# Query weights loaded in pieces of 32 partitions by 2048 columns in place of 128 partitions by 512 columns

## The reference

```
h = x + W_out(concat[A, B, C, D](rmsnorm(x) @ W_in))
x = h + PEER(rmsnorm(h));   y = rmsnorm(x)
```

```
q  = (x @ wq).reshape(n, 8, 2, 128)             # wq is 1024 x 2048
s1 = q[:, :, 0] . k1 ; s2 = q[:, :, 1] . k2     # 128 keys per half and head
# top 16 of each half, top 16 of the 256 sums -> 16 experts per token and head, softmax gates
out[t] = sum_s g[s] * gelu(u_tab[e[s]] . x[t]) * v_tab[e[s]]     # 16384 experts
```

## Time and profile before

| | |
|---|---|
| median of three runs | 1734.4 us (1732.55 to 1735.49) |
| the profiled execution, time of the whole run | 1734.5 us |
| its span | 1732.7 us |
| mean granted TensorE clock | 0.843 of full speed |
| VectorE busy | 1241.3 us, 72% |
| TensorE matmul busy | 1232.9 us, 71% |
| POOL busy | 910.8 us, 53% |
| ScalarE busy | 698.0 us, 40% |
| moved by DMA | 602.42 MB, mean 348 GB/s |

### The profile page before, as it was taken

One profiled execution on the slowest core, in us unless ns is written; L12 is line 12 of the kernel. 1 busy time (PEld: TensorE's weight loads), 2 busy tenths in 40 slices (PEclk: granted clock), 3 DMA queues, 4 the chain that ended last, 5 costly groups with the idle time before them and its releaser, 6 DMA issues.

```text
span 1732.7 us, 19380 instructions
## 1 busy us (share of the span) xinstructions
PE 1232.9 (71%) x5360; PEld 619.5 (36%) x5360; DVE 1241.3 (72%) x2955; ACT 698.0 (40%) x1986; POOL 910.8 (53%) x1134
## 2 busy tenths in 40 slices
PE   5997898567777767767976767675766667666555
PEld 4886766322333333322322323232322222222110
DVE  3568755688887877768586778676767777767774
ACT  3321113455444444334345445343433343434444
POOL 0155120467576566555366656555656655656762
PEclk9999899778899898878986778778888887768878
DMA  6321147999999999999799999999999999999996
GB/s 173 122 98 49 37 137 100 318 390 418 414 415 416 407 418 419 417 417 398 255 388 417 419 417 416 417 378 418 419 417 418 418 418 412 409 417 402 420 415 255
DMA packets 110636, 602.42 MB, mean 348 GB/s; under 512 B 24752, under 2 KB 27184, under 8 KB 43968
## 3 DMA queue, kind: packets, MB, share of 16 engines
q0 software_dynamic: 74880, 545.29, 76.8%
q1 hardware_dynamic: 35648, 55.90, 11.0%
HBM read 597.96 MB, written 3.19 MB: 347 GB/s over the span
## 4 chain that ended last, share of the span: by engine, by line
DMA 39%; PE 27%; DVE 15%; POOL 6%; ACT 5%; issue 5%; DVEq 3%; POOLq 0%; SPq 0%; ACTq 0%
DMA arena<-in_uv,arena 38%; PE ps L985 10%; DVE arena L1848 8%; PE ps L553 5%; POOL arena L2072 4%; DVE arena L1320 3%; DVEq L1317 3%; PE ps L600 2%; POOL arena L2071 2%; PE ps L906 2%; PE ps L591 2%; DVE arena L1326 2%; PE ps L613 1%; PE ps L925 1%; ACT arena L1284 1%
## 5 line engine op out<-in xcount | busy, mean ns | idle before, releaser
L985 PE MATMUL ps<-arena 128*64 128x512 f32 x2048 | 662.8, 782 | 407.9 <-ACT arena L1284 407.7
L1848 DVE CUSTOM_DVE_ANT_0 arena<-arena 128x1024 f32<-128x1024 f32 x520 | 641.0, 1234 | 303.8 <-DMA arena<-in_uv,arena 285.0
L2072 POOL DMA_INDIRECT arena<-in_uv,arena x520 | 622.7, 1198 | 90.5 <-POOL arena L2071 8.7
L2071 POOL TENSOR_TENSOR arena<-arena 1x1 f32<-1x1 f32 x520 | 207.1, 398 | 534.9 <-PE ps L985 404.8
L985 PEld LDWEIGHTS ps<-arena 128*64 128x64 f32 x2048 | 152.1, 166 | 798.2 <-ACT arena L1284 553.2
L1278 ACT ACTIVATE arena<-arena 128x1 f32<-128x1 f32 x520 | 105.3, 202 | 757.3 <-DVE arena L1848 755.8
L1284 ACT ACTIVATE arena<-arena 128x64 f32<-128x64 f32 (+1 forms) x520 | 181.5, 349 | 17.0
L1280 ACT ACTIVATE arena<-arena 128x1 f32<-128x1 f32 x520 | 153.2, 295 | 16.9
L1320 DVE TENSOR_TENSOR arena<-arena 128x512 f32<-128x512 f32 (+7 forms) x310 | 132.6, 429 | 28.1 <-ACT arena L1032 18.9
L553 PE MATMUL ps<-arena 128*128 128x264 f32 (+1 forms) x608 | 141.9, 389 | 0.7 <-DVE arena L1320 0.7
L906 PEld LDWEIGHTS ps<-arena 128*128 128x128 f32 x1024 | 121.9, 198 | 34.9 <-issue 33.4
(11 more groups left out here) (161 smaller groups left out, 973.8 us busy)
## 6 DMA issues: line engine op xcount, KB each, us to landing
arena<-in_win SPq DMA_DIRECT2D x38, 512.0 KB, 3.3
arena<-in_wqk SPq DMA_DIRECT2D x64, 256.0 KB, 7.5
arena<-in_uv,arena POOLq DMA_INDIRECT x520, 12.3
arena<-in_wout SPq DMA_DIRECT2D x16, 512.0 KB, 7.8
arena<-in_xp SPq DMA_DIRECT2D x4, 512.0 KB, 7.5
arena<-in_wqk SPq DMA_DIRECT2D x16, 128.0 KB, 9.5
out_yp<-arena SPq DMA_DIRECT2D x4, 512.0 KB
arena<-in_const SPq DMA_DIRECT2D x1, 928.0 KB, 4.5
```

The lines of the kernel that those rows point to most:

```text
L985: last = mm(ps[64 * q:64 * q + 64, b + c, :], diag[:, (s + q) % 8, :], ring[:, (s + q) % RING, D + 512 * c:D + 512 * c + 512], start=(s == ...
L1848: v.tensor_tensor_reduce(out=ring[:, s % RING, 0:D], in0=ring[:, s % RING, 0:D], in1=row, scale=1.0, scalar=0.0, op0=MUL, op1=ADD, accum_o ...
L2071: pool.tensor_tensor(carrier[:, 1:2], carrier[:, 0:1], carrier[:, 0:1], ALU.add).then_inc(S["carried"], 1)
L2072: pool.indirect_dma_start(out=ring[:, s % RING, :], out_offset=None, in_=a["uv"][:, :], in_offset=bass.IndirectOffsetOnAxis(ap=idx[:, t, s ...
```

## The change

A piece is now 32 partitions with all 2048 columns. It was 128 partitions with 512 columns. The number of pieces (4 per load), their bytes (256 KB), the waits before each and the semaphore counts are as they were, and so is the DMA of the keys.

```diff
@@ L465, load 0
             for k in range(4):
-                sp_.dma_start(wqk[:, 512 * k:512 * k + 512], a["wqk"][0][:, 512 * k:512 * k + 512]).then_inc(d_wqk, 16)
+                sp_.dma_start(wqk[32 * k:32 * k + 32, 0:2048], a["wqk"][0][32 * k:32 * k + 32, 0:2048]).then_inc(d_wqk, 16)
@@ L490, loads 1 to 15, in next_keys(n)
                     if u >= LEAD:
                         sp_.wait_ge(S["slot_used"], TOPK * (u - LEAD) + 2 + 2 * k)
-                    sp_.dma_start(wqk[:, 512 * k:512 * k + 512], a["wqk"][QLOADS[n]][:, 512 * k:512 * k + 512]).then_inc(d_wqk, 16)
+                    sp_.dma_start(wqk[32 * k:32 * k + 32, 0:2048], a["wqk"][QLOADS[n]][32 * k:32 * k + 32, 0:2048]).then_inc(d_wqk, 16)
```

## The result

The changed kernel takes 1789.66 us (median of 4 runs, 1786.59 to 1794.9) against 1734.95 us beside it. The ratio is 1.0312, 95% interval 1.0278 to 1.0347. The forecast was 1746 us with a range up to 1763 us. The direction was right and the size was not: 55 us were lost where 12 were forecast.

The account below looks back on a forecast made before the run. DMA engine time was taken to bound the kernel in the gather stretches. From 1734.5 us, - 3 for packets and + 15 for collisions gave 1746.5, stated as 1746 us; the 8-in-10 range was 1730 to 1763 us.

Parts of the forecast that it names:

- What bounds the kernel: Over 310 to 820 and 850 to 1650 us, DMA engine time added or saved moves the end one for one.
- Issue: The same 60 instructions of 0.33 us on the mostly idle SP queue behind the same waits: nothing either way.
- the wait for the weights: Queries waiting for a load: a piece would have to land 12 us later to be felt, so nothing.
- load 0: Issued at 245.0 to 246.7 us, before the first gather, its first product 31 us later: costed at nothing.
- Packets: Weight pieces as 32 runs of 8 KB instead of 128 of 2 KB, 6144 fewer packets: 3 us saved.
- The near row: Rate beside a load, 414 and 415 against 419 GB/s: 0.30 us lost per load, 4.5 us for 15.
- Collisions: DMA engines writing into the same 32 partitions hinder each other: 0.25 us per piece, 15 us for 60.
- half rate: Each of a DMA engine's two packets per piece takes 0.32 us more: 0.64 us per piece, 38 us for 15 loads.
- The signs: If pieces cost, stretches with a load fall to about 400 GB/s, the mean over 850 to 1650 us to about 405.
- full collisions: Rival: every packet of a piece, and gather packets into those partitions, at half rate: + 38 - 3, 1769 us; chance 0.09.
- The row of `ys`: Output at the end, 8 rows of 4 KB: 0.48 us per packet against 0.161 for `yp`, read as engines obstructing each other.
- only half of the DMA engines carry a piece: Rival: eight engines get four packets each, the lag hidden by waiting gathers: 1731.5 us; 0.32 together with the other no-collision rival.

Follow-up runs that it names:

- Half of the narrow loads: Changed kernel with narrow 32-partition pieces only in loads with odd n, the others as before the change: 1763.12 us, ratio 1.0151 to the kernel before.
- load 0 alone: Only the first load, issued before any gather, uses the narrow pieces; the other 15 are as in the kernel before: 1738.31 us, ratio 1.0004.
- spread kernel: Changed kernel with each piece on every fourth partition instead of 32 neighbours: 1734.26 us, ratio 0.9982 to the kernel before; again in 12 runs 1734.61 us, 0.9979.
- alternating order: Changed kernel with the four pieces of a load in the order 0, 2, 1, 3: 1786.9 us, ratio 1.0275 to the kernel before.

## Why the prediction was wrong, step by step

**What bounds the kernel: right.** DMA engine time in these stretches goes to the end one for one. 40.6 + 15.3 = 55.9 us more per engine stand beside 57.5 us more span, and the 51.4 us lost behind the loads beside 51.3 us more from the first gather to the last. Half of the narrow loads gave half of the loss, and the one outside the gathers gave none that shows.

**Issue, the wait for the weights, load 0: right to within what can be measured.** No query waited for its load, and load 0 alone changed no time. It was put at nothing because its own product starts late enough. What stood behind it in the queue was not looked at: TensorE waited 1.4 us for a block of `wout`, and the first gather came 61.1 us behind load 0, not 59.0. The reading that all 60 pieces lie in the bound stretches was too wide as well: load 1 is issued from 304.5 us, and load 7, at 809.84 us, reaches into the gap from 820 to 850 us. In the 28 us behind its first issue load 7 lost only 0.4 us more than before.

**Packets: the size came out, the reason is not shown.** 3 us saved, 4.5 at most, was the forecast. The spread kernel, which has the change's packets without its narrow target, gave 0.9982 and 0.9979, 3.1 and 3.7 us. The near row, the load's own stretch, was the one to use; the mean over the queue's packets would have said 15 us. But the run with one DMA of 1 MB has the same row packets and gave 0.9992 (0.9981 to 1.0003), so that the packets alone made the 3 us is not settled.

**Collisions: they are there, but only the smaller part of them was priced.** The step that failed is the sentence from half rate to the sum: "so about half of the time, 0.32 us per piece; the gathers still get every engine meanwhile". It priced only the packets of the pieces. For these its 15 us, 0.25 us per piece, are near what was measured. The loads' queue took 15.3 us more than before, packets saved included, and 20.8 us, 0.35 us per piece, more than in the spread kernel, which has the same packets. The gathers did not get off free. They lost 40.6 us per engine against the kernel before and 37.2 us against the spread one, 0.6 to 0.7 us per piece. That was put at nothing without a row for it. A gather has rows for every partition, so it too has to go in where the piece does; this is the likely reason, and no row shows a single packet waiting. The signs said the same: with a load the rate fell to 321 and 389 GB/s and not to about 400, and over 850 to 1650 us to 387 and not 405. What a piece costs beyond the spread version is (1.0312 - 0.9982) x 1735 / 60 = 0.95 us, where the forecast had 0.25.

**The upper bound was wrong for the same reason.** 38 us was called full collisions and was made of the two packets of a piece alone, though the rival's text spoke of the gather packets too. With as much again for gather packets the bound would have been 77 us, above the 55 us measured. As it was, the result lies 20 us beyond the 1769 us of full collisions, in the part above 1762 us that had a chance of 0.09.

**The row of `ys`** (three times as long for 4 KB packets at 8 partitions) pointed the right way. It is a transfer out of the on-chip memory and not into it, and no run varied it, so that it is slow for the same reason is not shown; in that the direction came out right there is some luck. The estimate from the Trainium skill's figure, in "SBUF — State Buffer", section "Door 1: The DMA port swizzle", was 36 us with nothing hidden: nearer than mine, and still short of the 55 us measured. It prices the piece and not its neighbours; whether that is the whole gap, no run shows.

**The rivals.** That only half of the DMA engines carry a piece would have cost nothing, and the time rules it out as forecast. Could it be the cause at a higher price? Rows that go to engines by partition might make much the same groups. But an engine without work would show as a lower DMA share, and the share stays at 1.02 while the rate falls to 321 GB/s; it is the packets that take longer, those of the gathers too. The alternating order, which would spread such a load better, changed nothing. This speaks against it and is not a proof. The loss is settled as one of the destination's partitions, paid mostly by the gathers. Two things stay open. No row shows which of the 16 DMA engines wrote which partition, so that two of them meet on one way is inferred from the groups and not seen. And the size is not derived: 0.95 us per 256 KB for the groups of 32, and (1.0626 - 0.9982) x 1739 / 60 = 1.87 us for 16 neighbours (1.8 us by the medians), a factor of 2 for half of the ways.

## What to carry to other kernels

Where a stream of transfers keeps the DMA engines full, a load beside it should put its bytes over all partitions in every piece. If rows are to be long and few, take every fourth partition and not a block of 32; every eighth was not enough. A block of 16 to 64 neighbours does not only take more DMA time itself, it slows down what runs beside it, and that part was two thirds to three quarters of the price here. The time to landing did not give it away: the median piece landed in 7.4 us, 7.5 us before. When a collision on a shared resource is priced, price both parties.

## What the runs showed of the hardware

- Beside a full stream of gathers, 256 KB into 32 or 64 neighbouring partitions, or in two DMAs into 16 that are eight apart, cost 0.9 to 1.0 us more than into every fourth partition; in two DMAs into 16 neighbours 1.8 to 1.9 us. At every second or fourth partition they cost no more than over all 128.
- The busy share does not show it: the DMA engines read 1.02 at 321 GB/s and 1.02 at 419 GB/s. The GB/s column has to be read with the share.
- With packets of 8 KB for 2 KB, 6144 fewer in all, the kernel of spread pieces was 3 to 4 us faster. The same row packets in one DMA of 1 MB gave a ratio of 0.9992 (0.9981 to 1.0003). Why that saves less was not tried.
